# A two-layer hybrid backbone on one core: retention's last store, the row maxima of attention and the first modulation stage

## The reference

```python
for i in range(DEPTH):                                   # 2 layers
    mx = split((silu(c) @ w_ada[i] + b_ada[i]), 6)       # modulations, for x; mc the same for ctx
    hx = modulate(rms_norm(x, norm1_w[i]), mx[0], mx[1]) # and hc
    ... = split_proj(hx, w_in[i])                        # one input projection, 21 tiles of 128
    # A: retention, 6 heads of 64, chunks of 128, both directions
    o_ret = silu(x_rg) * group_norm(bidir_retention(...))
    # B: latent attention, 4 heads of 96; C: grouped attention, 6 heads of 64, 2 key heads
    s = q @ k.T * scale; p = softmax(s); o = p @ v       # keys: 256 context + 1024 tokens
    x = x + mx[2] * (concat(o_ret, o_mla, o_gqa) @ w_out[i])
    x = x + mx[5] * conv_ffn(modulate(rms_norm(x, norm2_w[i]), mx[3], mx[4]))
return rms_norm(x, final_norm_w)
```

## Time and profile before

| | us |
|---|---|
| median of 3 runs (3586.6 to 3588.74) | 3587.6 |
| the profiled execution | 3586.47 |
| its span | 3584.6 |
| TensorE busy (matmul) | 3425.6 |
| TensorE busy (weight load) | 2915.6 |
| VectorE busy | 2373.2 |
| ScalarE busy | 1265.8 |
| GpSimd busy | 792.3 |

### The profile page before, as it was taken

One profiled execution on the slowest core, in us unless ns is written; L12 is line 12 of the kernel. 1 busy time (PEld: TensorE's weight loads), 2 busy tenths in 40 slices (PEclk: granted clock), 3 DMA queues, 4 the chain that ended last, 5 costly groups with the idle time before them and its releaser, 6 DMA issues. The chain is left out here.

```text
span 3584.6 us, 48645 instructions
## 1 busy us (share of the span) xinstructions
PE 3425.6 (96%) x18362; PEld 2915.6 (81%) x18362; DVE 2373.2 (66%) x3239; ACT 1265.8 (35%) x2135; POOL 792.3 (22%) x368
## 2 busy tenths in 40 slices
PE   7999889999989999999998899889999999999996
PEld 6888878888878888888887688779998788888884
DVE  7575556776178999989756533557883666666665
ACT  3331346677141111111222532356773322222222
POOL 3121210001322222222222211310013233232233
PEclk9999989999999999999999999999999999999998
DMA  5455462121112222222110324461212111111111
GB/s 220 138 182 191 138 197 65 53 57 59 48 57 83 72 75 70 70 70 70 36 40 25 144 103 150 138 201 38 55 52 77 43 47 47 47 50 50 41 47 47
DMA packets 95944, 304.19 MB, mean 85 GB/s; under 512 B 11584, under 2 KB 38336, under 8 KB 93632
## 3 DMA queue, kind: packets, MB, share of 16 engines
q1 hardware_dynamic: 95808, 302.33, 25.8%
HBM read 239.11 MB, written 63.18 MB: 84 GB/s over the span
## 5 line engine op out<-in xcount | busy, mean ns | idle before, releaser
L2057 DVE SCALAR_TENSOR_TENSOR xT<-down_acc,mod,xT 128x512 f32<-128x512 f32 (+1 forms) x840 | 541.7, 696 | 189.3 <-PE down_acc L183 186.9
L181 PE MATMUL up_acc<-h_hi,whi 128*128 128x512 f32 (+1 forms) x1720 | 637.5, 371 | 12.4 <-DVE h_lo L443 10.4
L182 PE MATMUL up_acc<-h_lo,whi 128*128 128x512 f32 (+1 forms) x1720 | 634.4, 369 | 0.0
L183 PE MATMUL up_acc<-h_hi,wlo 128*128 128x512 f32 (+1 forms) x1720 | 634.2, 369 | 0.0
L130 POOL TENSOR_TENSOR wlo<-raw,whi 128x1024 fp32r<-128x1024 f32 x133 | 339.2, 2551 | 1109.0 <-ACT whi L119 1109.0
L181 PEld LDWEIGHTS up_acc<-h_hi,whi 128*128 128x128 f32 x1720 | 325.4, 189 | 72.8 <-issue 10.3
L183 PEld LDWEIGHTS up_acc<-h_hi,wlo 128*128 128x128 f32 x1720 | 325.0, 189 | 54.2
L182 PEld LDWEIGHTS up_acc<-h_lo,whi 128*128 128x128 f32 x1720 | 325.4, 189 | 52.5
L1214 DVE TENSOR_REDUCE negmax<-scores 128x1 f32<-128x1280 f32 (+1 forms) x180 | 247.1, 1373 | 163.2 <-PE scores L1090 163.2
L1949 ACT ACTIVATE up<-up_acc 128x512 f32<-128x512 f32 (+1 forms) x210 | 115.8, 554 | 610.0 <-PE up_acc L183 610.0
L183 PE MATMUL down_acc<-hid_hi,first_wlo 128*128 128x512 f32 (+1 forms) x840 | 321.3, 383 | 0.0
(11 more groups left out here) (272 smaller groups left out, 6313.9 us busy)
## 6 DMA issues: line engine op xcount, KB each, us to landing
raw<-in_w_rest SPq DMA_DIRECT2D x112, 512.0 KB, 3.5
norm_buf<-in_w_ada SPq DMA_DIRECT2D x52, 768.0 KB, 4.5
first_raw<-in_w_rest SPq DMA_DIRECT2D x57, 512.0 KB, 3.6
proj_scratch<-stage SPq DMA_DIRECT2D x18, 640.0 KB, 3.6
raw<-in_w_first SPq DMA_DIRECT2D x21, 512.0 KB, 6.3
ada_raw<-in_w_ada SPq DMA_DIRECT2D x6, 1536.0 KB, 14.2
xT<-proj_scratch SPq DMA_DIRECT2D x4, 1920.0 KB, 8.4
xT<-in_xT SPq DMA_DIRECT2D x8, 640.0 KB, 19.2
```

The costliest lines, as they stand in the source:

```text
L181: nc.tensor.matmul(out, hi, xhi, start=start, stop=False)
L182: nc.tensor.matmul(out, hi, xlo, start=False, stop=False)
L183: return nc.tensor.matmul(out, lo, xhi, start=False, stop=stop)
L2057: nc.vector.scalar_tensor_tensor(xs, db[g % DB][:, :w], mod_of(layer, 5, m, c), xs, ALU.mult, ALU.add).then_inc(added, 1)
```

## The change

There are three independent edits and a small one.

1. SP issues retention's last store after head 0's values and ahead of the other heads' values and `fetch(1)`.
2. `roots` is split in `log` and `root`. For the last turn, the second layer runs `log` before `exp(0)` and `root` after it; the first layer runs both after `high(0)`.
3. The maximum of a whole step is taken in two parts: over columns 0 to 511 as soon as the scores' first piece is there (`s_first`), right after `low` of two steps before, and over the other 768 when all are there. A third instruction takes the smaller of the two negated values. The reciprocal moves behind `low`'s subtractions.
4. In the first stage TensorE takes five slabs and VectorE one (slab 1). TensorE holds the 2 columns of `cs` as weights and moves 384 columns of the slab, 8 products a slab, into two rows of PSUM. VectorE copies the rows to SBUF, and TensorE turns them into columns with products with a 2 x 2 identity, ahead of the totals. All squares are added by VectorE, the last in three chunks; GpSimd adds none. SP's order is slab 0, constants, slabs 1, 2, two weight units, slabs 3, 4, 5, the tokens, the third weight unit.

```diff
         groups = FIRST // 3
-        by_pe, by_dve = (0, 1, 2), (3, 4, 5)
...
             acc = s.sb("ada_acc", [P, len(by_dve), 2, GRP])
-            sq, odd = [s.sb(f"sq{i}", [P, TOK]) for i in range(4)], s.sb("odd_sum", [P, TOK])
+            row = s.sb("ada_row", [2, len(by_pe), GRP])
+            sq = [s.sb(f"sq{i}", [P, TOK]) for i in range(4)]
...
                 slab(0)
+                for dst, src in ((ident[:, :], "ident"), (ones_d[:, :], "ones_d"), (normw[:, :, :], "norm_w")):
+                    sp.dma_start(dst, a[src]).then_inc(small_in, 16)
+                slab(1)
                 sp.dma_start(bada[:, :, :], a["b_ada"]).then_inc(bias_in, 16)
-                for n in (3, 1, 4):
+                slab(2)
+                ring.loads(sp, 0, AHEAD)
+                for n in range(3, groups):
                     slab(n)
-                for k in range(KB // 2):
+                for k in range(KB):
                     tokens(k)
-                slab(2)
-                slab(5)
-                for dst, src in ((ones_d[:, :], "ones_d"), (normw[:, :, :], "norm_w"), (ident[:, :], "ident")):
-                    sp.dma_start(dst, a[src]).then_inc(small_in, 16)
-                for k in range(KB // 2, KB):
-                    tokens(k)
-                ring.loads(sp, 0, RING)
+                ring.loads(sp, AHEAD, RING)
...
-                for i, k in enumerate((2, 4, 6)):
-                    pool.wait_ge(sq_ready, k + 1)
-                    if i:
-                        pool.wait_ge(even_added, i)
-                    nc.gpsimd.tensor_tensor(sums, sums, sq[k % 4][:, :], ALU.add).then_inc(even_added, 1)
                 ring.los(pool, 0, AHEAD)
...
-                for k in range(KB):
-                    dst = sums if k == 0 else odd[:, :] if k == 1 else sq[k % 4][:, :]
-                    act.wait_ge(xin[k], 16)
-                    if k == 6:
-                        act.wait_ge(even_added, 1)
-                    elif k == 7:
-                        act.wait_ge(odd_added, 1)
-                    nc.scalar.activation(dst, xT[:, k, :], ACT.Square).then_inc(sq_ready, 1)
                 for u in range(AHEAD):
                     ring.split_hi(act, 0, 0, u)
+                for k in range(KB):
+                    dst = sums if k == 0 else sq[k % 4][:, :]
+                    act.wait_ge(xin[k], 16)
+                    if k > 4:
+                        act.wait_ge(added, k - 4)
+                    if k < KB - 1:
+                        nc.scalar.activation(dst, xT[:, k, :], ACT.Square).then_inc(sq_ready, 1)
+                    else:
+                        for t0, w in CHUNKS:
+                            nc.scalar.activation(dst[:, t0:t0 + w], xT[:, k, t0:t0 + w], ACT.Square).then_inc(sq_ready, 1)
...
-                pe.wait_ge(silu_done, 1)
-                for n, d in zip(by_pe, by_dve):
+                def rows_of(i):
+                    n = by_pe[i]
                     pe.wait_ge(loaded[n], 16)
+                    if i >= 4:
+                        pe.wait_ge(row_copied, i - 3)
+                    for kb in range(KB):
+                        mm = nc.tensor.matmul(rows[i % 4][0:2, :GRP], cs[:, kb, :], raw[:, n, kb, :], start=(kb == 0), stop=(kb == KB - 1))
+                    mm.then_inc(row_done, 1)
+                def turn_rows(i):
+                    pe.wait_ge(row_copied, i + 1)
                     for f in range(3):
-                        at = 2 * (3 * n + f)
-                        for kb in range(KB):
-                            mm = nc.tensor.matmul(bank[:, at:at + 2], raw[:, n, kb, f * P:(f + 1) * P], cs[:, kb, :],
-                                                  start=(kb == 0), stop=(kb == KB - 1))
-                    mm.then_inc(tiles, 1)
-                    pe.wait_ge(summed, d - by_dve[0] + 1)
+                        at = 2 * (3 * by_pe[i] + f)
+                        mm = nc.tensor.matmul(bank[:, at:at + 2], row[:, i, f * P:(f + 1) * P], ident[0:2, 0:2], start=True, stop=True)
+                    mm.then_inc(turned, 1)
...
+                pe.wait_ge(silu_done, 1)
+                for i in range(len(by_pe)):
+                    rows_of(i)
                 pe.wait_ge(small_in, 48)
+                for i in range(len(by_dve)):
+                    sum_partitions(i)
+                for i in range(len(by_pe)):
+                    turn_rows(i)
                 for i, (t0, w) in enumerate(CHUNKS):
-                    pe.wait_ge(joined, i + 1)
+                    pe.wait_ge(added, KB - 1 + i)
                     nc.tensor.matmul(totals[i][:, :w], ones_d[:, :], sums[:, t0:t0 + w], start=True, stop=True).then_inc(total_done, 1)
...
-                def add_odd(k):
+                def copy_rows(i):
+                    dve.wait_ge(row_done, i + 1)
+                    nc.vector.tensor_copy(row[:, i, :], rows[i % 4][0:2, :GRP]).then_inc(row_copied, 1)
+                def add(k):
                     dve.wait_ge(sq_ready, k + 1)
-                    if k > 3:
-                        dve.wait_ge(odd_added, k // 2 - 1)
-                    nc.vector.tensor_tensor(odd[:, :], odd[:, :], sq[k % 4][:, :], ALU.add).then_inc(odd_added, 1)
-                multiply(3)
-                multiply(4)
-                add_odd(3)
-                multiply(5)
-                add_odd(5)
-                add_odd(7)
-                dve.wait_ge(even_added, 3)
-                dve.wait_ge(odd_added, 3)
-                for t0, w in CHUNKS:
-                    nc.vector.tensor_tensor(sums[:, t0:t0 + w], sums[:, t0:t0 + w], odd[:, t0:t0 + w], ALU.add).then_inc(joined, 1)
+                    if k > 1:
+                        dve.wait_ge(added, k - 1)
+                    nc.vector.tensor_tensor(sums, sums, sq[k % 4][:, :], ALU.add).then_inc(added, 1)
+                multiply(0)
+                for i in range(3):
+                    copy_rows(i)
+                for k in range(1, 4):
+                    add(k)
+                copy_rows(3)
+                for k in range(4, 6):
+                    add(k)
+                copy_rows(4)
+                add(KB - 2)
+                for i, (t0, w) in enumerate(CHUNKS):
+                    dve.wait_ge(sq_ready, KB + i)
+                    if i == 0:
+                        dve.wait_ge(added, KB - 2)
+                    nc.vector.tensor_tensor(sums[:, t0:t0 + w], sums[:, t0:t0 + w], sq[(KB - 1) % 4][:, t0:t0 + w], ALU.add).then_inc(added, 1)
                 dve.wait_ge(bias_in, 16)
-                dve.wait_ge(tiles, groups)
+                dve.wait_ge(tiles, len(by_dve))
+                dve.wait_ge(turned, len(by_pe))
...
                 sp.wait_ge(ret.main_done, ret.turns)
                 sp.dma_start(mvs[:, :, 0, :].bitcast(f32), mv_d[:, :, 0, :]).then_inc(mv_first, 16)
+                ret.store(sp, ret.turns - 1)
                 sp.dma_start(mvs[:, :, 1:, :].bitcast(f32), mv_d[:, :, 1:, :]).then_inc(mv_in, 16)
                 fetch(1)
-                ret.store(sp, ret.turns - 1)
...
                             mm = nc.tensor.matmul(S[n % 2][:, c0:c0 + w], q[:, b * P:(b + 1) * P], k[:, c0:c0 + w],
                                                   start=(x == 0), stop=(x == len(terms(h)) - 1))
+                        if p == 0 and not is_ctx(n):
+                            mm.then_inc(s_first, 1)
                     mm.then_inc(s_done, 1)
...
+                if last:
+                    ret.log(act, ret.turns - 1)
                 exp(0)
-                ret.roots(act, ret.turns - 1)
+                if last:
+                    ret.root(act, ret.turns - 1)
                 for n in range(N + FLUSH0 + NP):
                     if n < N:
                         high(n)
+                    if n == 0 and not last:
+                        ret.log(act, ret.turns - 1)
+                        ret.root(act, ret.turns - 1)
...
+                def first_part(n):
+                    if not is_ctx(n):
+                        dve.wait_ge(s_first, whole[n] + 1)
+                        nc.vector.tensor_reduce(first_max[:, n:n + 1], S[n % 2][:, :512], AX.X, ALU.max, negate=True).then_inc(part_done, 1)
                 def maximum(n):
                     dve.wait_ge(s_done, n + 1)
-                    nc.vector.tensor_reduce(negmax[:, n:n + 1], S[n % 2][:, :CTX if is_ctx(n) else TOK], AX.X, ALU.max,
-                                            negate=True).then_inc(max_done, 1)
+                    top = negmax[:, n:n + 1]
+                    if is_ctx(n):
+                        nc.vector.tensor_reduce(top, S[n % 2][:, :CTX], AX.X, ALU.max, negate=True).then_inc(max_done, 1)
+                        return
+                    nc.vector.tensor_reduce(top, S[n % 2][:, 512:TOK], AX.X, ALU.max, negate=True).then_inc(rest_done, 1)
+                    dve.wait_ge(part_done, whole[n] + 1)
+                    dve.wait_ge(rest_done, whole[n] + 1)
```

(16 more changed lines are left out.)

33 lines of the change are left out of this document (21 added, 12 removed).

## The result

The changed kernel takes 3547.48 us (median of 4 runs, 3543.9 to 3549.22) against 3587.86 for the kernel before on the same chip: ratio 0.9883, 95% interval 0.9871 to 0.9896, so 40.4 us faster where 49.8 were forecast. Its profiled execution took 3543.9 us (span 3542.1, before 3584.6): 42.5 us less. It was the shortest of the four; on another chip four more runs gave 3547.84 to 3550.72.

What follows compares the result with a forecast made beforehand. TensorE's waits for `ptl`, the idle starts of attention and the first stage's late sum were taken as the limits. Transitions 18.2, maxima 21.9 and first stage 9.7 sum to 49.8 us, giving a median of 3538; range 3527 to 3565.

Steps and rivals of the forecast that it cites:

- Store: Starts of both attentions: retention's last store ahead of the loads ends TensorE's idle time, 9.6 and 6.9 us.
- Logarithm and root: Starts of both attentions: moving the two activations around the first exponential gains 0.4 us in the first layer, 1.3 in the second.
- First stage: First stage: five slabs on TensorE at the fast pace, last additions done at 46.5 in place of 56.26, gain 9.7 us.
- rival of slow row products: First stage: row products stay at 10.4 us a slab, stage ends 7 us later than before, 3555; chance 0.13.
- Maxima: Attention in both layers: row maxima in two parts let `low` start sooner, 21.9 us, bounds 8 and 27.
- 48 pairs at 0.30: Grouped attention, both layers: each pair of steps loses 0.30 us of TensorE's waiting, 14.4 us.
- 32 pairs at 0.14: Latent attention: each pair of steps gains 0.14 us, 4.5 us in all.
- ten changes of head: First layer: `low` waits for a whole maximum after a short context step; about 0.3 us each, 3.0 in all.
- The sign that was named for it: Attention: TensorE's waits for `ptl` fall from tens of microseconds to a few if the forecast is right.
- The reciprocal: VectorE in attention: moving it behind `low` costs nothing, as it is read a step later.
- The slower rival: Every whole step of attention: VectorE becomes the bound at 4.09 us a step, 38 us lost, 3598; chance 0.04.
- the bounds 0 and 0.2: VectorE, between the second part of the maximum and the minimum: a gap in us, taken as 0.05.

Runs made afterwards that it cites:

- the kernel without hits: The changed kernel with the minimum of the two parts as a reduction over two adjacent columns: 3544.37 us against 3548.86 for the changed kernel beside it.

## Why the forecast was right in sign and 9 us too good

**Store.** Right, and at its size. Forecast 9.6 + 6.9, by undoing it 10.5 + 6.3. The prediction's times for `out_done` (500.6 and 2377.6, in the time of the kernel before) fit: shifted by the 9.5 and 31.5 us that the starts came sooner they are 491.1 and 2346.1, and the store was issued at 490.56 and 2346.50. The loads behind SP's wait delayed nothing. One sentence was too sure: that the granted clock doesn't fall again. `finish` delays `low(1)`, TensorE idles 2.10 us, and in this trace the clock was 0.50 from 494 to 496. It cost 0.8 us: start 1 took 15.00 to 15.07 in three traces with the fall, 14.28 to 14.29 in four without. The prediction named TensorE itself as the next thing late, and not `finish`, which the change didn't move but which now stood behind a first part; the 1.1 us of VectorE in front of `low(1)` were in the rows.

**Logarithm and root.** Perhaps too low: forecast 0.4 + 1.3, undoing them costs 1.6 + 2.5 in the trace, of which a part is the fall of the clock, and 1.8 by the medians. How much of the trace's figure is the order of the two operations and how much the clock is not shown.

**First stage.** Right, at 9.5 for 9.7, with the last additions at 46.6 (forecast 46.5) and products 0.66 apart (0.65). The prediction's reading, that the old stage ran at the 1.2 GHz pace whatever its record says, is borne out: the record is missing there, and products of one form change their pace where it begins. Its reason for taking the fast pace, that the new products move 384 columns, came out too, but only from 12.6 us on. The first slab ran at the slow pace up to there, which cost nothing, since TensorE waited for the loads of the next ones (0.46 and 0.92 us). The rival of slow row products didn't happen beyond that. The five slabs as column products show what it would have cost: not 7 us over the kernel before, as the rival said, but 8.5 (the first exponential at 503.48 for 495.02).

**Maxima.** This is the step that failed: "48 pairs at 0.30 ..., 32 pairs at 0.14 ..., ten changes of head", 21.9 us. The changed kernel's rests are 12.9 us shorter. That is inside the bounds of 8 and 27 that the term was given, though the hits were no part of their reasoning. The sign that was named for it, waits for `ptl` down to a few microseconds, failed as well: 37.9 of the 62.0 us are left, and 34.7 in the kernel without hits. The parts:

- *One pair stood for 48.* The earlier trace rows is a plain pair. Of the eight pairs of two heads, three also transpose finished outputs; there TensorE has more of its own work and less waiting. Plain pairs went from 7.70 to 7.47, not 7.40; the other three from 7.65, 7.96 and 7.92 to 7.53, 7.73 and 7.80 (spacing of exponentials 140 to 156 in the kernel with the minimum as a reduction, which is free of hits). That is 1.6 us per eight pairs where 2.4 were taken, 9.7 over 48 (an estimate) instead of 14.4. Latent pairs gave more, 8.73 to 8.50, since the one wait of 0.17 in the earlier trace rows wasn't all of theirs.
- *Without hits* the two rests are 16.9 us shorter (345.38 and 297.31 against 354.97 and 304.60). So 5.0 of the 9.0 missing are pairs and changes of head. By place, 10.4 of the 16.9 lie in the grouped heads and 6.5 in the latent ones. The forecast had 14.4 and 4.5 for their pairs alone, and the 3.0 for the ten changes of head on top, for which these sums leave no room; the changes by themselves were not measured.
- *The hits of GpSimd* are the other 4.0 (346.75 + 299.88 less 345.38 + 297.31). The prediction priced the new minimum at 0.15 us and looked for its dangers in VectorE's own queue, though the earlier trace rows already held the mechanism: additions of two SBUF operands that ran at a third of their pace beside GpSimd's split. The rows had shown that VectorE and GpSimd block each other, and the minimum was a new operation of that very kind. The Trainium skill (SBUF — State Buffer, Who interferes with whom) states it: an instruction of VectorE with two SBUF inputs contends with one of GpSimd that reads SBUF, and a reduction never does. Both halves agree with the rows here: 1.76 us against 0.16 in the one form, 0.159 at most in the other.

**The reciprocal** "costs nothing, it is read a step later": true of where it went, wrong of where it stood. Alone it is worth 4.7 us by the median and 5.7 in the rests. The sum didn't miss them, since the 1.48 from maximum to `low` held the reciprocal, but they went to the account of the maxima: two parts alone, with the reciprocal left ahead of `low`, give 14.1 of the 16.9.

**The slower rival.** VectorE didn't become the bound. The wait behind the reduction is 0.10 us (it lasts 0.96, and the minimum starts 1.05 after it did, under 1.1 in 157 of 160 steps, 1.4 in three), between the bounds 0 and 0.2 and twice the 0.05 taken. The advice of the Trainium skill (VectorE: DVE Perf Modes, Rules for kernel authors) on the number of operations, weighed in the prediction, decided nothing: two more instructions a step left TensorE the bound of a pair.

**What moved on its own.** The stretch between the attentions gave 1.8 us more than nothing and the end took 1.4 back. In the other traces they range from 1492.8 to 1496.2 and from 884.7 to 888.7. For the end the place is visible, a stretch of the last products over the tokens, before and after:

```profile
3559.00:3563.00 4.00, 3.28 (x8) 1.14 (x6) 0.00 (x0) 0.69 (x1) 0.00 (x0) 1.00 0.00 0
```

```profile
3515.00:3519.00 4.00, 4.00 (x7) 1.74 (x6) 0.00 (x0) 0.00 (x0) 0.00 (x0) 0.61 0.00 0
```

The granted clock is 1.00 in one and 0.61 in the other, with the same instructions after the same pause of 2.66 us. The stretch to the first exponential has such a place too. It ends at 485.2 to 485.6 in six traces with the changed stage and at 486.8 to 487.4 in four, and from 404 us on, behind a pause of TensorE, the clock is low for longer in the late ones (the minimum as a reduction, then with the reciprocal ahead):

```profile
404.00:414.00 10.00, 8.46 (x37) 7.79 (x38) 5.13 (x9) 5.22 (x17) 9.16 (x4) 0.50 0.07 11
```

```profile
404.00:414.00 10.00, 7.44 (x50) 6.88 (x50) 5.10 (x9) 6.07 (x20) 8.68 (x4) 0.83 0.01 3
```

Instruction by instruction on VectorE the first of these two is 0.5 us ahead at 400 us and 1.6 behind at 424, and from there to the first exponential. Of the 1.8 us between the attentions 1.1 appear around a stretch where TensorE's clock is low for longer before (0.76 from 1070 to 1084 us) than after (0.88 from 1042 to 1056). That the clock is their cause is likely and not shown, and where the rest lies stays open.

## What to carry to other kernels

Before a small operation is added to an engine, ask not only what queues behind it but where its operands lie and who else reads there: here 160 minima of 0.16 us cost 4 to 8 us because a handful met GpSimd's subtractions, and the same minimum in another form cost nothing. Price a repeated gain by every kind of step that repeats, not by the step with the largest wait. When a part is credited with a gain, undo exactly that part: the reordered reciprocal, priced at zero, carried 5.7 us with one maximum and 2.8 of the 16.9 with two parts. And before a clock is read from a profile, look whether it was recorded there at all: the same product at two paces tells more.

## What the runs showed of the hardware that was not expected

- A minimum of one column with both operands in SBUF is held until GpSimd's subtraction ends (33 of 33, 0.16 us elsewhere and up to 2.80, the longest in the kernel with column products); a reduction of two columns in the same place is not (0.154 to 0.159, 160 times in each trace, 30 of them in five traces beside such a subtraction). `low`, with one operand in PSUM, isn't held either; the kernel before shows its three pieces at their usual length beside the same subtraction:

```profile
2552.38 1.60 DVE L1232 TENSOR_TENSOR ptl<-scores,pth 128x512 fp32r<-128x512 f32 x3
...
2552.56 2.40 POOL L1065 TENSOR_TENSOR first_wlo<-first_raw,first_whi 128x1024 fp32r<-128x1024 f32 x1
```

- Column products ran for 51 us without a pause at 0.214 us a pass, twice the 0.11 of retention's passes in the earlier trace rows, and passes of 1 column right behind them took 2.70 us for twelve where 1.50 is the figure in the changed kernel: the engine was busy and still at its 1.2 GHz level. Row products of 384 columns had left that level 4.6 us after they began. The profile prints 1.00 in both cases, since its records begin only with the first change.
- Whether the clock falls in a pause of about 2 us differs between executions: for the wait in start 1 (2.10 us) it fell to 0.50 in the changed kernel's first trace and stayed at 1.00 in its second.
